# Moving the sample group's depthwise taps of a two-layer decoder step from TensorE and VectorE to a GpSimd product and a VectorE sum

## The reference, cut to what matters

```python
def conv_module(z, buf, dw, dw_b, ln_g, ln_b):
    u = z[..., :CONV_CH] * jax.nn.sigmoid(z[..., CONV_CH:])
    u_full = jnp.concatenate([buf.astype(u.dtype), u], axis=1)   # buf: the last 30 rows (zeros for the prompt)
    y = lax.conv_general_dilated(u_full, dw[:, None, :], (1,), 'VALID', ..., feature_group_count=CONV_CH) + dw_b
    y = jax.nn.silu(layernorm(y, ln_g, ln_b))
    return y, u_full[:, -(CONV_WIDTH - 1):]
```

## Time and profile before

| | |
|---|---|
| median of 3 runs | 2062.93 us (2059.91 to 2064.4) |
| the profiled execution's own time | 2061.77 us |
| its span, first to last instruction | 2060.1 us |
| busy share of the span: PE, DVE, ACT, POOL | 89%, 47%, 26%, 6% |
| mean granted TensorE clock, share of full speed | 0.942 |
| the chain that ended last, by engine | PE 77%, DVE 14%, ACT 4% |

### The profile page before, as it was taken

The page is one execution under the profiler, slowest core; times in us unless marked ns, Lnnn a source line. Parts: engine busy times, 40 slices in busy tenths (PEclk is TensorE's granted clock), DMA queues, the critical chain, the costliest instruction groups (busy, mean ns, idle before and its releaser), DMA issues.

```text
span 2060.1 us, 36026 instructions
## 1 busy us (share of the span) xinstructions
PE 1828.9 (89%) x13959; PEld 1588.1 (77%) x13959; DVE 964.4 (47%) x1532; ACT 541.7 (26%) x901; POOL 125.8 (6%) x267
## 2 busy tenths in 40 slices
PE   5999565899999999799877898988979899999998
PEld 4876434889999999799754555555549799999997
DVE  5397875443333222477554655566533533333222
ACT  3211223232222211243321333333322322222110
POOL 1000000000000000244210000000000000000000
PEclk9999866999999999999986999999989999999999
DMA  3211121222222322223352577777862122223221
GB/s 116 62 42 31 31 88 47 76 62 82 83 84 84 94 85 76 67 67 79 99 173 65 161 246 245 246 246 256 266 220 82 57 83 84 83 82 93 75 84 60
DMA packets 239464, 224.68 MB, mean 109 GB/s; under 512 B 12114, under 2 KB 199588, under 8 KB 239354
## 3 DMA queue, kind: packets, MB, share of 16 engines
q1 hardware_dynamic: 229168, 200.83, 31.9%
q0 software_dynamic: 8768, 19.09, 2.9%
q10 hardware_dynamic: 1418, 3.29, 0.5%
HBM read 215.37 MB, written 7.80 MB: 108 GB/s over the span
## 4 chain that ended last, share of the span: by engine, by line
PE 77%; DVE 14%; ACT 4%; issue 2%; DMA 1%; ACTq 0%; SPq 0%; DVEq 0%; POOL 0%
PE ps L1461 55%; PE ps L1816 4%; PE ps L1651 3%; PE ps L1832 2%; PE ps L1863 2%; PE ps L1443 1%; DVE tmp L419 1%; PE ps L1837 1%; DVE yc L698 1%; PE ps L1907 1%; DVE aL L423 1%; DVE prob L921 1%; DVE rb L429 1%; DVE rb L414 1%; PE ps L1923 1%
## 5 line engine op out<-in xcount | busy, mean ns | idle before, releaser
L1461 PE MATMUL ps<-aH,wH 128*128 128x288 f32 x2224 | 488.1, 301 | 50.0 <-DVE aL L423 34.5
L1461 PE MATMUL ps<-aL,wH 128*128 128x288 f32 x2224 | 480.9, 298 | 0.0
L1461 PE MATMUL ps<-aH,wL 128*128 128x288 f32 x2224 | 480.8, 298 | 0.0
L1461 PEld LDWEIGHTS ps<-aH,wH 128*128 128x128 f32 x2224 | 362.7, 191 | 59.3 <-issue 35.6
L400 DVE TENSOR_TENSOR wL<-raw,wH 128x1024 fp32r<-128x1024 f32 (+1 forms) x179 | 232.0, 1296 | 339.2 <-ACT wH L1063 336.1
L1461 PEld LDWEIGHTS ps<-aH,wL 128*128 128x128 f32 x2224 | 363.0, 191 | 0.0
L1461 PEld LDWEIGHTS ps<-aL,wH 128*128 128x128 f32 x2224 | 363.0, 191 | 0.0
L1063 ACT ACTIVATE wH<-raw 128x1024 fp32r<-128x1024 f32 (+1 forms) x179 | 199.0, 1112 | 409.2 <-PE ps L1461 359.6
L1461 PE MATMUL ps<-gH,wH 128*128 128x288 f32 x704 | 151.9, 297 | 4.8 <-DVE gL L616 4.8
L1461 PE MATMUL ps<-gH,wL 128*128 128x288 f32 x704 | 151.6, 296 | 0.0
L1461 PE MATMUL ps<-gL,wH 128*128 128x288 f32 x704 | 151.6, 296 | 0.0
(11 more groups left out here) (302 smaller groups left out, 1916.4 us busy)
## 6 DMA issues: line engine op xcount, KB each, us to landing
kring<-in_cache_fox_k_dram SPq DMA_DIRECT2D x128, 384.0 KB, 3.8
vring<-in_cache_fox_v_dram SPq DMA_DIRECT2D x128, 384.0 KB, 4.0
raw<-in_w_gate_up_dram SPq DMA_DIRECT2D x88, 512.0 KB, 3.7
raw<-in_w_down_dram SPq DMA_DIRECT2D x32, 704.0 KB, 4.5
raw<-in_fox_w_in_dram SPq DMA_DIRECT2D x21, 512.0 KB, 3.9
raw<-in_w_out_dram SPq DMA_DIRECT2D x16, 512.0 KB, 3.7
raw<-in_conv_w_in_dram SPq DMA_DIRECT2D x14, 512.0 KB, 3.8
raw<-in_w_mem_kv_dram SPq DMA_DIRECT2D x8, 512.0 KB, 3.6
```

Of the source, the lines that this page charges most:

```text
L1461: mm = nc.tensor.matmul(ps[:, 2 * slot + h, 0:HT], weights[:, w], a[:, k0 + k, h * HT:(h + 1) * HT], start=(first and k == 0 and weights i ...
```

## The change

Sample tokens no longer go through PE's taps, ACT's copy or DVE's steps. For each channel tile GpSimd multiplies a window view of `uS` (8 sequences x 8 tokens x 31 taps, overlapping) with the weights into a new buffer `uw` of 8 x 8 x 32, and copies the bias into the last of the 32 places. DVE sums the 32 places into `yc` with one `tensor_reduce`, issued ahead of the third step of the tile's chain. `uw` is one buffer, laid over `prob` and `pT`: the product of a tile waits until the sum of the tile before is done, the sum waits for its product. The prompt steps wait for the step right before them instead of the one before that. GpSimd issues the diagonals of tiles 0 and 1 first, and then, in each pass, those of tile c + 2 and the product of tile c.

```diff
+        uw, _ = at("uw", [P, NB, NQ, W + 1], o)
         mb0, _, o0 = memory_buffers(0, o, None, None)
...
-                    sj = uS[:, c, :, j:j + NQ].rearrange("p o b n -> p (o b) n")
-                    yp, ysm = y[:, 0:SEQ], y[:, SEQ:T].rearrange("p (b n) -> p b n", b=NB)
+                    yp = y[:, 0:SEQ]
+                    if j == begin + 2:
+                        dve.wait_ge(uw_done, c0 + 1 + 2 * i)
+                        nc.vector.tensor_reduce(y[:, SEQ:T], uw[:].rearrange("p b q w -> p (b q) w"), AX_X, ALU.add).then_inc(uw_used, 1)
                     if j > begin:
-                        dve.wait_ge(vchain, steps.value() - 1)
-                    steps.inc(nc.vector.scalar_tensor_tensor(out=yp, in0=uj, scalar=w, in1=yp, op0=ALU.mult, op1=ALU.add))
-                    if j > begin:
-                        dve.wait_ge(vchain, steps.value() - 1)
-                    last = nc.vector.scalar_tensor_tensor(out=ysm, in0=sj, scalar=w, in1=ysm, op0=ALU.mult, op1=ALU.add)
+                        dve.wait_ge(vchain, steps.value())
+                    last = nc.vector.scalar_tensor_tensor(out=yp, in0=uj, scalar=w, in1=yp, op0=ALU.mult, op1=ALU.add)
...
-                steps.enter(i, 4 * (W - PE_TAPS))
+                steps.enter(i, 2 * (W - PE_TAPS))
...
-                nc.scalar.activation(y[:, 0:SEQ], ps[:, 4 * (c0 % 2), 0:SEQ], ACT.Identity, bias=bias)
-                nc.scalar.activation(y[:, SEQ:T], ps[:, 4 * (c0 % 2) + 1, 0:NS], ACT.Identity, bias=bias).then_inc(y_begun, 1)
+                nc.scalar.activation(y[:, 0:SEQ], ps[:, 4 * (c0 % 2), 0:SEQ], ACT.Identity, bias=bias).then_inc(y_begun, 1)
...
-                    nc.tensor.matmul(ps[:, 4 * (c0 % 2), 0:SEQ], w, uj, start=(j == 0), stop=(j == n - 1))
-                    mm = nc.tensor.matmul(ps[:, 4 * (c0 % 2) + 1, 0:NS].rearrange("p (b n) -> p b n", b=NB), w, sj,
-                                          start=(j == 0), stop=(j == n - 1))
+                    mm = nc.tensor.matmul(ps[:, 4 * (c0 % 2), 0:SEQ], w, uj, start=(j == 0), stop=(j == n - 1))
...
+            def sample_windows(c):
+                pool.wait_ge(u_done, c + 1)
+                if c:
+                    pool.wait_ge(uw_used, c)
+                x = uS[:, c, :, 0:NQ]
+                windows = bass.AP(tensor=x.tensor, offset=x.offset, ap=[list(x.ap[0]), list(x.ap[1]), [1, NQ], [1, W]])
+                nc.gpsimd.tensor_tensor(uw[:, :, :, 0:W], windows, dw[:, c, :].unsqueeze(1).unsqueeze(1).broadcast_to([P, NB, NQ, W]),
+                                        ALU.mult)
+                bias = vec[:, V_DWB + c:V_DWB + c + 1].unsqueeze(2).broadcast_to([P, NB, NQ])
+                last = nc.gpsimd.tensor_copy(uw[:, :, :, W:W + 1].rearrange("p b q o -> p b (q o)"), bias)
+                last.then_inc(uw_done, 1)
+            for c in range(2):
+                diagonals(c)
             for c in range(KC):
-                diagonals(c)
+                if c + 2 < KC:
+                    diagonals(c + 2)
+                sample_windows(c)
```

More of the change, by code:

```diff
@@ L244, in build @@
         yc, o = at("yc", [P, KC, T], o)
+        uw, _ = at("uw", [P, NB, NQ, W + 1], o)
         mb0, _, o0 = memory_buffers(0, o, None, None)
+        assert NB * NQ * (W + 1) <= 2 * 2 * NM + 2 * 4 * P
         ks_at = o0 - 3 * 4 * GS * MT * MW
@@ L344, in build @@
         diag_ready, taps_ready, y_begun = sem("diag_ready"), sem("taps_ready"), sem("y_begun")
+        uw_done, uw_used = sem("uw_done"), sem("uw_used")
         ysq_used, swish_done, usc_done = sem("ysq_used"), sem("swish_done"), sem("usc_done")
```

## The result

Six runs of the changed kernel have a median of 2072.57 us (2069.8 to 2074.23), six of the kernel before 2061.17 us: the ratio is 1.0055, with a 95% interval of 1.0043 to 1.0066. A ratio here is taken from the fast runs of its set and need not be the quotient of the medians beside it (1.0042 in the second set). The kernel is slower, by about half a per cent. The forecast was 2074 us. Its size was met partly by luck, as the comparison of the stages will show.

The account below looks back on a forecast made before the run. Bound: PE's taps up to DVE's lo at 213.49, DVE after; DVE's tile 5 glu, delayed by GpSimd's products, gates PE. 9.6 + 2.2 = +11.8 us on 2061.77 gives 2073.6, predicted median 2074; 8-in-10 range 2065 to 2081.

Parts of the forecast that it names:

- PE and ACT: Convolution taps: each 0.22 us shorter, 14 us over 64 taps; ACT's dropped copy 0.2 us; PE alone about 15 us sooner.
- DVE's steps: Removing sample steps gives 0 in the 92 looped steps (pitch 0.90); written-out steps gain 0.08 us each.
- The sum: DVE's tensor_reduce per tile: 2.27 us long, 2.0 us added in each looped tile and in tiles 4 and 5.
- The product's own price: GpSimd's product takes 4.2 us (ends 2.1 and 7.7) and holds DVE up for its whole length, W.
- Glu of tile 5: DVE's glu gating PE's last taps starts at 101.1 + 77.4 + 3 x 2.0 + 3W = 197.1, 13.5 us later.
- The wait and its clock: PE, free near 189, waits some 9 us before tile 5's taps, then restarts at half clock, losing 2.5 us.
- The joint: DVE's step behind the lo it idles for, at 214.63 before: 7.1 us later plus 2.5 for the clock, 9.6.
- Behind the joint: Tile 4's opening +1.75, product 5 on the first reciprocal +0.6, twelve faster steps -1.0, tile 5 +0.8: +2.2 us.
- No hold-up: Rival 1: products do not hold DVE up (W = 0); kernel ends 3.9 us earlier, 2059.0; chance about 0.09.
- The one-pass product: Rival 2: GpSimd's product is one pass, W = 2.1 us; +5.3 us, 2068; chance 0.2.
- the slow one: Rival 3: GpSimd's product takes 7.7 us; +25 us, 2088; chance 0.1.
- The looped pitch: Rival 4: DVE's looped steps fall to 0.79 us apart; -8.8 on the forecast, +3, 2066; chance 0.06.

Follow-up runs that it names:

- second set: Both kernels run again unedited: the changed kernel 2069.19 us, ratio 1.0035; the kernel before 2061.82 us, ratio 1.0011.
- experiment 4: Kernel before without PE's sample taps and ACT's sample copy, DVE's sample steps kept, GpSimd zeroing the samples' part once: 2052.95 us, ratio 0.9956.
- experiment 2: Changed kernel with DVE's sum covering only the last two of the 32 places: 2060.09 us, ratio 0.9998 to the kernel before.
- experiments 1 and 3: experiment 1, and the changed kernel with GpSimd making each product twice: the latter 2080.85 us, ratio 1.0092 to the kernel before.
- experiment 1: Changed kernel with GpSimd's product made for tile 0 only, sums and bias copies kept: 2060.51 us, ratio 0.999 to the kernel before.
- experiment 6: Kernel before with only PE's sample taps moved, to ACT as one activation each, DVE summing them and keeping its sample steps: 2052.3 us, ratio 0.9957.

## Why the prediction was right, step by step

**What bounds it: right.** The clause that it said decides the case (DVE becomes what PE waits for) is what happened. DVE's idle ahead of the lo fell from 17.40 us to 7.97, and PE now waits for DVE three times for a lo and once for the glu.

**PE and ACT: right.** In experiment 4 the joint moves by 10.7 us with DVE's work unchanged. It is less than the 14 us of taps because the glu of tile 5 then stands in the way: it comes only 4.4 us sooner, and PE waits 2.6 us for it.

**DVE's steps: right, in both kinds.** Twelve looped steps take 10.59 us in the changed kernel, a pitch of 0.894; the sample steps in the gaps had been free. Twelve written-out steps take 9.40, a pitch of 0.79.

**The sum: right.** 2.28 us for the instruction, 2.0 net behind the joint (experiment 2); where it stands in the loop, 1.84.

**The product's own price: right to 1%; what it costs DVE: 15% too large.** It takes 4.16 us alone, and 4.2 was the estimate from two streamed operands. The Trainium skill, page "GPSIMD Engine Reference", section "Elementwise — side-by-side cycle accounting", gives 4497 ns for an add of 2048 fp32 elements; the estimate of 4.4 from it is 6% above the product measured here. The step that failed is "I charge a product its own length". Beside DVE the product is 4.51 us long, of which 3.65 are lost (experiments 1 and 3). The rest is hidden: 0.52 us under the end of the step in flight, 0.13 in the gap that DVE has after a step anyway, and the held step ends 0.54 us behind the product and not its full 0.75. The bias copy, charged against that gap, cost nothing: the next step starts 0.15 us behind the held one, as without it. So DVE does stand still until the product is done, but the loss lies between the prediction's two prices, 4.2 by the whole length and 3.2 by the share of 0.82/1.09. The mistakes were to take the hidden part for 0.27 us whatever the length (against 4.16 it is 0.51) and to let the copy use it up.

**Glu of tile 5: 197.1 predicted, 193.1 measured.** The products explain 3 x 0.55 = 1.7 of the 4.0 us and the sums 3 x 0.16 = 0.5. The other 1.8 lie in the base of 77.4 us; with no product (experiment 1) the stretch from the glu of tile 2 to that of tile 5 took 80.5 us, and 83.4 was the forecast for it with three sums. A part of this can be read from rows: the last step of a run has no gap behind it, so the sample step that followed it was not free there, some 0.2 us at six places. This was argued and not tried by itself. Product 4 was put into DVE's wait for its lo; it ran from 199.68 beside nine steps that took 11.48 us, but 7.97 us of that wait were left behind them, so it cost nothing, as priced.

**The wait and its clock: mechanism right, wait too large.** PE's wait for the glu was 5.4 us and not 9, since the glu came sooner. From the glu to the joint there are 26.9 us; the forecast has 24.6 and 2.5 for the clock. The taps' 16.24 instead of 13.8 us are that 2.5, within 0.1. PE was free for them at 188.65, where the forecast has 189. What the clock costs does not follow from the wait's length alone: PE waits 2.6 us for the glu in experiments 1 and 4 alike, and then the 16 taps take 15.70 us in experiment 1, with the granted clock at 0.50 for part of them, and 14.00 in experiment 4, at 1.00 throughout.

**The joint: +9.6 predicted, +5.4 measured.** That is the glu's 4.0 us again, and 0.2 in the stretch behind it.

**Behind the joint: +2.2 predicted, +1.3 measured.** Two sums and faster steps, as costed. Product 5 was given 0.6 us; the reciprocal beside it took its 3.75, and the multiplication behind it 0.92 instead of 0.82, so it cost 0.1. That is 0.5 of the 0.9; where the other 0.4 lies was not separated.

**The sum of it: +11.8 predicted, +6.7 at the stage's end, +12.0 at the span's.** "Everything after 272 us follows in a row and shifts with it" is the sentence that was wrong the other way. It did not shift as a block: up to the residual, in the memory attention, 2.9 us more came in the first pair of profiles and 2.2 in the second. Behind the residual it was +2.4 in the first pair and -1.5 in the second, which does not repeat. So two errors met: a convolution term 5.1 us too large, and 2 to 3 us behind the stage that the sum put at nothing. The rest of the agreement with +12.0 is luck. The medians of the two sets, 2072.6 and 2069.2, with +11.3 and +7.2 us by their ratios, lie on the lower side of the forecast's centre. (The prediction's own addition, 2073.6 and 1.2, gives 2074.8, where it says 2074.)

**The rivals.** No hold-up is refuted by the step of 4.40 us; its time, 2059.0, is near what experiment 1 shows (2060.51) when the product is gone, though that kernel also pays 1.7 us for a lower clock under its taps (15.70 against 14.00) and 2 to 3 us for the longer stretch behind the stage, which the rival left out. The one-pass product is refuted by 4.16 us, the slow one too. The looped pitch did not fall. That GpSimd's early diagonals matter by themselves was not tried.

What stays open: what puts a kernel into the upper or the lower group between the stage's end and the residual, some 3 us apart for the same work; no run isolates it. The profiled execution of experiment 6 (2047.6 us) is 4.7 us under the median of its runs, so the median is the number to use. Its trace shows where it was short: 1694.2 us behind the residual, where the others have 1696.8 to 1703.5.

## What to carry to other kernels

Before moving work to GpSimd beside a DVE that is nearly full, charge DVE's two-input instructions with the length of the GpSimd instruction, less what is hidden under the step in flight and the gap behind it: here 3.65 us for 4.51, three times in a row on the chain. Work that sat in a gap (a second chain of steps between two links of the first) was free here, and taking it away gave nothing; what PE shed was worth 9 us, and ScalarE could carry it at 0.25 us a tap with no standstill. And when a change ends ahead of a stretch whose clock rises and falls, as here, allow some 3 us either way for that stretch until the end is measured, and profile both kernels twice to see which part comes again.

## What the runs showed of the hardware

The hold-up between the two engines works both ways: a GpSimd product that starts under a DVE step is longer (4.44 to 4.67 us in the changed kernel against 4.16 alone), and the next DVE instruction with two SBUF inputs waits for its end (a step of 4.40 us instead of 0.75, a lo of 5.17 instead of 1.22), while a reciprocal with one input runs at its 3.75 us beside it. ScalarE's products beside DVE steps (experiment 6, tile 4) lengthened neither.

The granted clock of the memory attention, work that no kernel here touches, differed from kernel to kernel and between two profiles of one, and not in step with the time (33.0 us at 0.69 and 33.7 at 0.80 in the kernel before). From the stage's end to the residual six profiles took 88.4 to 89.6 us and four 91.5 to 91.8, and the changed kernel's two agree. Behind the residual one kernel's two profiles differ by 4 us, so an effect of 0.1 to 0.2% of this kernel is not shown by one profile.
